# Finishing the GELU of the expert dots on ScalarE, and adding VectorE's own share of the values one step later

## What is computed

```python
u = jnp.take(u_tab, i_i, axis=0)
a = jax.nn.gelu(jnp.einsum('td,thkd->thk', x_i, u))
return jnp.einsum('thk,thkd->td', a * g_i, jnp.take(v_tab, i_i, axis=0))
```

## Time and profile before

| | |
|---|---|
| median of 3 runs | 4896.7 us (4895.64 to 4897.29) |
| the profiled execution, its own time | 4901.72 us |
| its span, first to last instruction | 4899.9 us |
| mean granted TensorE clock | 0.91 |
| busy: PE, DVE, ACT, POOL | 79%, 71%, 18%, 35% of the span |
| bytes moved | 1585.74 MB, mean 324 GB/s |

### The profile page before, as it was taken

The page is one execution under the profiler, slowest core; times in us unless marked ns, Lnnn a source line. Parts: engine busy times, 40 slices in busy tenths (PEclk is TensorE's granted clock), DMA queues, the critical chain, the costliest instruction groups (busy, mean ns, idle before and its releaser), DMA issues.

```text
span 4899.9 us, 40501 instructions
## 1 busy us (share of the span) xinstructions
PE 3853.5 (79%) x12130; PEld 1993.8 (41%) x12130; DVE 3457.3 (71%) x9187; ACT 873.7 (18%) x2482; POOL 1704.5 (35%) x1515
## 2 busy tenths in 40 slices
PE   7887889697977677768777679799787777777776
PEld 4546474345433233324443346446443333232222
DVE  2323788857889967776678778867787777766665
ACT  2311241101111122111111123110111111111111
POOL 2330132332234433444334323234134444443332
PEclk8988989899999888988988889899999889999999
DMA  7665467765689999999999667767479999999998
GB/s 267 209 219 196 155 250 271 273 253 214 228 357 393 367 385 400 413 405 398 407 421 416 263 226 261 292 237 278 168 272 398 409 406 410 406 413 422 421 421 345
DMA packets 228951, 1585.74 MB, mean 324 GB/s; under 512 B 27302, under 2 KB 29650, under 8 KB 42620
## 3 DMA queue, kind: packets, MB, share of 16 engines
q0 software_dynamic: 198016, 1395.87, 71.6%
q1 hardware_dynamic: 30716, 187.28, 9.9%
HBM read 1571.74 MB, written 11.30 MB: 323 GB/s over the span
## 4 chain that ended last, share of the span: by engine, by line
DMA 20%; PE 18%; DVE 13%; issue 4%; ACT 2%; POOL 1%; DVEq 0%; POOLq 0%; ACTq 0%
DMA sb_arena<-in_peer_uv,sb_idx 12%; PE ps L1123 10%; DMA sb_gbufs<-in_peer_uv,sb_idx 8%; PE ps L1022 4%; DVE sb_gbufs L1903 3%; DVE sb_arena L1903 2%; DVE sb_eacc L1926 1%; PE ps L737 1%; PE ps L1060 1%; POOL sb_gbufs L2145 1%; DMA sb_ring<-in_w_oab 1%; ACT sb_dge L1390 1%; PE ps L880 1%; DVE sb_arena L1889 1%; POOL sb_arena L2145 1%
## 5 line engine op out<-in xcount | busy, mean ns | idle before, releaser
L2145 POOL DMA_INDIRECT sb_gbufs<-in_peer_uv,sb_idx x768 | 947.0, 1233 | 1863.4 <-PE ps L1123 815.1
L1123 PE MATMUL ps<-sb_gbufs,sb_dge 128*128 128x512 f32 x1856 | 933.9, 655 | 317.6 <-ACT sb_dge L1390 317.5
L1123 PE MATMUL ps<-sb_arena,sb_dge 128*128 128x512 f32 x1856 | 930.4, 653 | 316.5 <-ACT sb_dge L1390 316.3
L2145 POOL DMA_INDIRECT sb_arena<-in_peer_uv,sb_idx x512 | 558.8, 1091 | 846.1 <-PE ps L1123 809.8
L1903 DVE CUSTOM_DVE_ANT_0 sb_gbufs<-sb_gbufs,sb_keep 128x1024 f32<-128x1024 f32 x512 | 620.4, 1226 | 272.3 <-DMA sb_gbufs<-in_peer_uv,sb_idx 270.7
L1903 DVE CUSTOM_DVE_ANT_0 sb_arena<-sb_arena,sb_keep 128x1024 f32<-128x1024 f32 x512 | 619.2, 1224 | 253.9 <-DMA sb_arena<-in_peer_uv,sb_idx 252.1
L1123 PEld LDWEIGHTS ps<-sb_gbufs,sb_dge 128*128 128x128 f32 x1856 | 373.2, 209 | 853.1 <-issue 445.4
L1123 PEld LDWEIGHTS ps<-sb_arena,sb_dge 128*128 128x128 f32 x1856 | 371.2, 208 | 848.0 <-ACT sb_dge L1390 442.5
L1385 ACT ACTIVATE sb_small<-sb_small 128x2 f32<-128x2 f32 x512 | 104.2, 203 | 2156.4 <-DVE sb_small L1914 2156.4
L1926 DVE SCALAR_TENSOR_TENSOR sb_eacc<-sb_gbufs,sb_small,sb_eacc 128x1024 f32<-128x1024 f32 x299 | 388.1, 1298 | 9.4 <-DVE sb_small L1937 0.6
L1390 ACT ACTIVATE sb_dge<-sb_ident,sb_small 128x128 f32<-128x128 f32 x928 | 327.2, 395 | 123.5 <-DVE sb_small L2000 122.8
(11 more groups left out here) (270 smaller groups left out, 4323.5 us busy)
## 6 DMA issues: line engine op xcount, KB each, us to landing
sb_ring<-in_w_wq SPq DMA_DIRECT2D x32, 1024.0 KB, 6.9
sb_keep<-in_w_ada POOLq DMA_DIRECT2D x52, 512.0 KB, 6.4
sb_ring<-in_w_hy SPq DMA_DIRECT2D x24, 1024.0 KB, 7.5
sb_ring<-in_w_ga SPq DMA_DIRECT2D x16, 1024.0 KB, 8.2
sb_ring<-in_w_gb SPq DMA_DIRECT2D x16, 1024.0 KB, 9.4
sb_ring<-in_w_oab SPq DMA_DIRECT2D x16, 1024.0 KB, 8.8
sb_ring<-in_w_out SPq DMA_DIRECT2D x14, 1024.0 KB, 8.9
sb_gbufs<-in_peer_uv,sb_idx POOLq DMA_INDIRECT x768, 10.7
```

Of the source, the lines that this page charges most:

```text
L1123: q = pe.matmul(ps[:, c, :], dge[:, b, :], gbuf[b][:, D + c * 512:D + c * 512 + 512], start=(h == 0 and i == 0), stop=(h == HALVES - 1 and ...
L2145: nc.gpsimd.indirect_dma_start(out=gbuf[b], out_offset=None, in_=I["peer_uv"], in_offset=bass.IndirectOffsetOnAxis(ap=idx[:, col:col + 1], ...
```

## The change

ScalarE now makes the whole weight but for the product of dot and routing weight. The dot is scaled by C where it is summed. ScalarE squares a pair of dots (one 128 x 2 operation), then takes two tanh, one for each expert of the pair, of dots * (A d^2) + dots, where both the factor and the addend are columns read from memory; then two Identity activations make tanh * gated + gated, which is the weight. VectorE keeps the product with the routing weight (`gated_dots`) and loses the two operations for the argument and the one that made the weight. The factor 0.5 / C is in the routing weights.

In the prompt group VectorE's `finish_pair` waits for the weights of ScalarE (`w_ready`). In the latent tiles VectorE waits for nothing of ScalarE except before it adds a kept value; and it adds the kept value of step m behind the dots of step m+1 (`add_kept`), where before it stood at the end of step m. At the first step of a tile the product with the routing weight now stands ahead of the end of the tile before (`add_experts`), not behind it.

```diff
+                def weight_of_pair(n, q):
+                    act.wait_ge(Z["ttr"], 2 * n)
+                    act.activation(dsq[:, q:q + 2], dots[:, q:q + 2], ACT.Square, scale=GELU_A ** 0.5 / GELU_C).then_inc(Z["sq"], 1)
+                    act.wait_ge(Z["sq"], n)
+                    for i in (q, q + 1):
+                        act.activation(dth[:, i:i + 1], dots[:, i:i + 1], ACT.Tanh, scale=dsq[:, i:i + 1], bias=dots[:, i:i + 1]).then_inc(Z["th_e"], 1)
+                    act.wait_ge(Z["gated"], n)
+                    act.wait_ge(Z["th_e"], 2 * n)
+                    for i in (q, q + 1):
+                        act.activation(dw[:, i:i + 1], dth[:, i:i + 1], ACT.Identity, scale=dgate[:, i:i + 1], bias=dgate[:, i:i + 1]).then_inc(Z["w_ready"], 1)
...
-                        act.wait_ge(Z["inner"], k0 + m + 1)
-                        act.activation(dth[:, q:q + 2], din[:, q:q + 2], ACT.Tanh, scale=GELU_C).then_inc(Z["th_e"], 1)
+                        weight_of_pair(k0 + m + 1, 2 * (m % 4))
...
-                    act.wait_ge(Z["inner"], k0 + m + 1)
-                    act.activation(dth[:, q:q + HALF], din[:, q:q + HALF], ACT.Tanh, scale=GELU_C).then_inc(Z["th_e"], 1)
-                    act.wait_ge(Z["w_ready"], layer * STEPS_S + m + 1)
+                    weight_of_pair(k0 + m + 1, q)
+                    act.wait_ge(Z["w_ready"], 2 * (k0 + m + 1))
...
-                dve.tensor_tensor_reduce(gbuf[b][:, 0:D], gbuf[b][:, 0:D], h2, 1.0, 0.0, ALU.mult, ALU.add,
+                dve.tensor_tensor_reduce(gbuf[b][:, 0:D], gbuf[b][:, 0:D], h2, GELU_C, 0.0, ALU.mult, ALU.add,
...
-                dve.scalar_tensor_tensor(out=cube, in0=dv, scalar=GELU_A, in1=dv, op0=ALU.mult, op1=ALU.mult).then_inc(Z["p_small"], 1)
...
-                dve.scalar_tensor_tensor(out=inn, in0=cube, scalar=1.0, in1=dv, op0=ALU.add, op1=ALU.mult).then_inc(Z["inner"], 1)
-                dve.tensor_tensor(dg, dv, gates, ALU.mult).then_inc(Z["p_small"], 1)
...
+                dve.wait_ge(Z["ttr"], 2 * n)
+                dve.tensor_tensor(dgate[:, q:q + 2], dots[:, q:q + 2], gates, ALU.mult).then_inc(Z["gated"], 1)
...
-                        dve.wait_ge(Z["th_e"], k0 + m + 1)
-                        dve.wait_ge(Z["p_small"], smalls[0])
-                        link(dve.scalar_tensor_tensor(out=dw[:, q:q + 2], in0=dth[:, q:q + 2], scalar=1.0, in1=dgate[:, q:q + 2], op0=ALU.add, op1=ALU.mult))
+                        dve.wait_ge(Z["w_ready"], 2 * (k0 + m + 1))
...
                     for i in range(HALF):
                         dot("s", layer, m * HALF + i, q + i, h2s[:, t - 1, :])
+                    gated_dots(k0 + m + 1, q, gwt[:, t * SLOTS + h * HALF:t * SLOTS + h * HALF + HALF])
+                    if m:
+                        add_kept(m - 1)
                     if h == 0 and t > 1:
                         add_experts(t - 1)
-                    gelu_argument(q, HALF, gwt[:, t * SLOTS + h * HALF:t * SLOTS + h * HALF + HALF])
-                    dve.wait_ge(Z["th_e"], k0 + m + 1)
```

More of the change, by code:

```diff
@@ L247, with pairs_before @@
 SLOT, OCCUPIED = expert_slots()
+def pairs_before(group, layer):
+    return layer * (PAIRS + STEPS_S) + (PAIRS if group == "s" else 0)
 def of_tile(layer, t, who):
@@ L505, in build @@
         dge = dgeflat[:, :].rearrange("p (n m) -> p n m", m=128)
-        dots, din, dth, dw, dgate, dcube = (small[:, 8 * i:8 * i + 8] for i in range(6))
+        dots, dsq, dth, dw, dgate = (small[:, 8 * i:8 * i + 8] for i in range(5))
         gbuf = [gbufs[:, i * 2 * D:(i + 1) * 2 * D] for i in range(4)] + [a(8192 + i * 2 * D, 2 * D) for i in range(4)]
```

44 lines of the change are left out of this document (16 added, 28 removed).

## The result

The changed kernel takes 4939.99 us (median of 5 runs, 4937.06 to 4956.69), the kernel before 4897.29 (5 runs, 4895.64 to 4908.9). The ratio is 1.0089, with a 95% interval of 1.0073 to 1.0105: **slower by 43 us**. The forecast was 4896, its range ended at 4931, and "slower" had a chance of 0.30. The profiled execution of after took 4948.3 us, its span is 4946.4; before it was 4901.7 with a span of 4899.9. The traces are therefore 46.5 us apart, 4 us more than the medians. One execution of experiment E3 took 6479 us and enters no ratio; all others of a kernel lie within 0.5% of each other.

The account below looks back on a forecast made before the run. Gathers bound the saturated latent tiles (ceiling 421 GB/s), VectorE bounds 1360 to 1720. Latent -34, prompt +30, last pair +1, kept values +2 make -1 us on the profiled 4901.7, which is 5.0 above the median: 4896 us, range 4862 to 4931.

Parts of the forecast that it names:

- the term for the prompt stages: Prompt stages: VectorE's additions wait longer for ScalarE's weight; 30 us on, from 16 to 56.
- the delay that was counted: Prompt pairs: 85 that waited for the tanh, each addition 0.78 us later, 66 us; the other 43 as nothing.
- ScalarE's holding: Prompt stages: ScalarE is held as long, its dense step queued behind the last Identity; no size given.
- the share on the path: Prompt stages: how much of the 66 us sets the end; at least 25%, at most 85%, 45% taken.
- The second rival: Prompt stages: the new wait replaces the removed one, most of it on the path; +33, 4930 us, chance 0.26.
- the latent gain: Latent tiles: VectorE saves 0.62 us a pair; 34 us off, from 15 to 55, 24 of it from 1360 to 1720.
- the cap: Latent tiles, 1360 to 1720: transfers can rise from 376 to 421 GB/s, so at most 38 us gained.
- ScalarE's chain: Each pair: 1.64 us from last sum to the weight's first use, 0.78 us longer than before (0.24 to 1.00).
- The later diagonal: Latent tiles: 0.78 us later, hidden in 6 us of gather queueing; costs nothing where transfers are full.
- The third rival: Latent tiles, layer 0: kept values free their buffers so late that gathers starve; +48, 4945 us, chance 0.04.
- the sign of the kept values: Latent tiles, 1720 to 2680: GB/s falling below 406 would show the kept values' cost.
- The first rival: Prompt delay mostly hidden, 16 us counts, latent stretches give 45; net -29 + 3, 4870 us, chance 0.34.

Follow-up runs that it names:

- E3: E1 with each kept value added at the end of its own step instead of the next; 4901.44 us, ratio 1.0003 to the kernel before.
- E2: The kernel before with only the prompt pairs changed, its latent tiles left as they were; 4963.69 us, ratio 1.0124 to the kernel before.
- E5: E1 with four one-column Identity operations on an unread tile behind each prompt tanh on ScalarE; 4904.45 us, ratio 1.0004 to the kernel before.
- E1: The kernel before with only the latent tiles changed, its prompt's small operations left as they were; 4886.37 us, ratio 0.9974 to the kernel before.
- E8: E1 with the prompt's small operations done value by value, ScalarE starting when each dot is there; 4878.07 us, ratio 0.9953 to the kernel before.
- E9: E8 with the prompt's product of dot and routing weight moved to ScalarE too; 4862.89 us, ratio 0.9928 to the kernel before.

## Why the prediction was wrong, step by step

**The step that failed** is the term for the prompt stages, "**30 us on**, from 16 to 56", of which E2 measured 61. Three things went into it.

First, the delay that was counted. 85 x 0.78 = 66 us left out what the prediction put at nothing: "In the other 43 pairs one dense operation or more stands between: ... I take them as nothing." In the traces the way from last sum to addition became 91 us longer in after than before, 68 of them in the 83 pairs with no dense work between and 23 in the 45 others (95 us in all in E2). The delay of a pair itself held, 0.86 against 0.78.

Second, ScalarE's holding. It was named in the prediction ("ScalarE is held as long, with its dense step queued behind the last Identity"), but no term was given to it. E5 puts it at about 14 of the 61 us.

Third, the share on the path: "I take 45%, nearer to the chain's row than to the busy share". With the holding in it, 61 of 95 us is 64%; with the 14 us taken apart it is half, and 45% can't be called wrong as a mean. 45% of 95 and 14 more are 57 us. What was wrong is to take one share for both stages from the chain of one stretch. By the starts of the gathers, worked out from the traces: "longer" is how much longer the way from sum to addition became, summed over the stretch's 16 pairs, and "later" how much the stretch of gathers grew, both in us.

| gathers of the prompt | starts before at, us | E2 over before: longer, later | after over E1: longer, later |
|---|---|---|---|
| 0 to 32 | 522 | 11.3, 11.2 | 9.7, 14.8 |
| 32 to 64 | 688 | 12.5, 5.9 | 14.1, 14.1 |
| 64 to 96 | 852 | 11.5, 4.8 | 12.1, 5.5 |
| 96 to 127 | 1028 | 10.6, 1.3 | 10.4, 0.5 |
| 640 to 672 | 2772 | 9.2, 6.8 | 9.1, 11.2 |
| 672 to 704 | 2942 | 16.5, 16.4 | 13.7, 9.4 |
| 704 to 736 | 3080 | 12.7, 3.1 | 12.7, 3.6 |
| 736 to 767 | 3276 | 10.3, 2.0 | 10.4, 1.2 |

The later additions are spread fairly evenly, and what they cost is not. In the first half of each stage nearly all of it counts (40 of 50 us in E2, 50 of 47 in after), in the second half a quarter (11 of 45 in both). The stretch of the earlier trace rows lies in a second half, and the 25% read from it hold for its own half. I had written that VectorE's share "must be larger there", in layer 0 from 740 to 980, and did not act on it. The busy share would not have told it either: from 3060 to 3300 VectorE is busy for 190 of 240 us before, 79%, and a quarter counts.

The second rival had the sign, the mechanism and in the main its place right. Its +50 and 4930 came near the measured 61 and 4940 in part by luck, since it took 75% of a delay that was nearly a third too small, and no holding.

**The second term that was mis-sized** is the latent gain: "**Sum: 34 us off**", of which 24 from 1360 to 1720. E1 measured 13 (trace: 15). The saving of VectorE was right: in after the read of the last sum ends at 1571.20 and the next work starts at 1571.32, 0.12 us later, as worked out. What was wrong is the cap. 376 GB/s as a mean of 360 us was read as a stretch in which every pair can gain up to 421. In E1 the pieces of 20 us are of several kinds (columns as in the earlier trace rows):

```profile
1380.00:1400.00 20.00, 15.97 (x36) 6.32 (x35) 13.82 (x52) 9.04 (x29) 9.94 (x9) 1.00 1.01 422
1400.00:1420.00 20.00, 10.13 (x19) 4.14 (x18) 19.18 (x67) 4.77 (x16) 4.70 (x4) 0.74 0.74 293
1420.00:1440.00 20.00, 13.28 (x25) 5.51 (x24) 19.48 (x69) 8.91 (x28) 7.26 (x6) 0.83 0.71 270
1440.00:1460.00 20.00, 17.47 (x36) 6.88 (x34) 11.71 (x44) 7.93 (x26) 10.27 (x10) 0.91 1.01 419
...
1560.00:1580.00 20.00, 14.67 (x30) 6.28 (x31) 19.69 (x28) 8.57 (x27) 7.74 (x8) 0.91 1.01 419
```

In the first and the fourth the link is full and VectorE has 6 to 8 us to spare: a saving there buys nothing. In the last both are full, and a saving can buy nothing there either. In the two between VectorE is full (19.2 and 19.5 of 20 us) with routing work, and only 4 and 6 gathers go out. The saving counts in such pieces, and few pairs fall there. The prediction said that saving and cap "don't fall on the same pairs" and still took 24 of 38; 12, its lower end, would have been about right: by the starts of the gathers, 160 to 288 (1378 to 1752 before) lie 12.6 us nearer together in E1 and 14.6 in after. The rest does not follow the forecast piece by piece. Gathers 128 to 160 come 4 us further apart in both, and from gather 1024 to the end both gain 4.8 us, where the forecast had nothing (E2, without the latent part, has 0.3 there); no run tells why. The sentence on VectorE's idle time there is too strong as well: the waits that it names are 24.6 of 36.8 us; and the highest slice of the earlier trace rows has 422, not 421, which changes no term. What it said would show the gain (the same gathers in some 336 us at about 400 GB/s) did not come: 372 GB/s in after, 379 in E1.

**What held.** ScalarE's chain: square 0.20, pairs of 0.67 and 0.66 (0.65 each had been taken), 1.72 us in all against 1.64, and 0.86 later against 0.78. The later diagonal in the saturated stage came out of the queueing of the gather, as worked out from the earlier trace rows. The chain there in after (the second Identity alone is on it):

```profile
4835.49 12.47 DMA sb_arena<-in_peer_uv,sb_idx
4847.98 1.22 DVE sb_arena L1916
4849.24 0.21 ACT sb_small L1370
4849.48 0.67 ACT sb_small L1373 x2
...
4850.53 0.38 ACT sb_small L1377
4850.93 0.41 ACT sb_dge L1403
4851.39 3.71 PE ps L1128 x8
...
4855.36 13.15 DMA sb_arena<-in_peer_uv,sb_idx
```

The landing takes 12.47 instead of 13.38 us, and from one gather to the next along the chain it is 19.87 us (4855.36 − 4835.49), where the trace of before has 19.93 (4803.57 to 4823.50). It is not a matter of single gathers: from 4380 to 4880 the median landing in `arena` is 12.4 us in E1 and 13.3 before. ScalarE did not become the bound in the latent tiles (222 of 500 us busy). The third rival, kept values that starve gathers, is out: adding them at once (E3) costs 14 us and wins nothing, and no wait of VectorE for ScalarE's weights is left from 1260 to 2740 in after. From 1720 to 2680 the transfers did fall below 406 GB/s, to 402, which the prediction had as the sign of the kept values; E1, which has them too, stands at 406 there, so it is not theirs. The first rival had one thing right, that a good part of the delay is hidden beside TensorE's work, but not its size.

Put together by the prediction's own terms: −13 instead of −34 + 2 + 1 for the latent part, +61 instead of +30 for the prompt, +48 against the +43 measured for the whole; the interval of the difference (36 to 51) holds it.

## What to carry to other kernels

When a change takes time from an engine but puts a wait for another engine into its queue, price the wait by how much later each dependent instruction comes (here 1.73 against 0.86 us), summed over all of them, those with a short operation between included. Then take the share that counts stretch by stretch: here it was nearly all in the first half of each stage and a quarter in the second, and neither the chain of one stretch nor the busy share gave the whole. Price the longer time that the other engine is held as a term of its own. A saving under a cap should be counted in pieces as long as the work between two bursts, since a mean bandwidth below the ceiling can be a mixture of pieces that are full and pieces that are bound elsewhere. And if small operations are moved, let each start when its own input is there (E8, E9) before asking whether the other engine is quick enough: taken pair by pair they cost 56 us over E1, and value by value they won 10 (E8), or 23 with the product moved too (E9).
